# Two weight slabs side by side at the start of every dense layer

## The chip, the cores and the metric

The kernel runs on one core of a Trainium2 chip. TensorE (PE) multiplies 128x128 tiles of weights with 128x512 tiles of activations and sums in PSUM banks; VectorE (DVE), ScalarE (ACT) and GpSimd (POOL) do the elementwise work; SyncE (SP) issues most of the transfers. The metric is the device time of one execution in microseconds (us), lower is better: the median of three runs.

## The reference, cut to what matters

A token mixer, an expert layer (PEER) and two further blocks follow each other on 512 tokens of width 1024. All but the expert layer are chains of "normalise, multiply with a weight matrix, elementwise work, add to the residual". The changed code is in the multiplications with a weight matrix:

```
a = rmsnorm(h, g_mix); z = a @ w_in                                  # w_in
h = h + concat([ya, yb, yc]) @ w_out                                 # w_out
gate = sigmoid(rmsnorm(h, g) @ w_gate); h = h + gate * (p @ w_proj)  # ple_a, ple0, ple1
u = rms_norm(x) @ ssm_w_in; ...; val, gate = split(g @ w_glu)        # ssm_in, glu
up = rms_norm(x) @ w_up; c = conv(up); x = x + (gelu(g) * val) @ w_down   # up0/down0, up1/down1
k, v = split(rms_norm(x, kv_norm) @ kv_w); q = rms_norm(x) @ w_q     # w_k, w_v, attn_q
x = x + o @ w_o                                                      # attn_o
```

## The kernel before, in words

Activations lie transposed in SBUF as eight tiles (KT = 8) of 128 features by 512 tokens. A weight matrix comes in slabs: one slab holds the weights of 128 output features, eight 128x128 tiles for a depth of 1024 (ten in the three `ple` layers, where two more tiles multiply the side input `p`). `LAYERS` lists 15 layers with their numbers of slabs, 226 slabs in all.

Products are made of half-precision parts. Every operand is split into an f16 part and a bf16 remainder, and each product of two tiles is three matmuls (`PARTS`), so a slab is 24 matmuls of 512 columns, 30 in a `ple` layer. VectorE splits the activations (`split_tile`, L1171 to L1176, called by `norm_tiles`, L1204, once per tile after scaling it; each finished tile counts up `a_ready` or `x_split`). GpSimd splits the weights (`split`, L1824): L1833 writes the f16 part, L1835 the remainder, and its drain at L1836 counts up `split_done`.

A slab goes through these stations: SyncE loads it into one of four places of `wring`; GpSimd splits it into one of two places of `wsp` (NSPLIT = 2); TensorE multiplies it into bank `t % 4`; ScalarE or VectorE reads the bank and counts up `evac_done`. What holds the order of GpSimd is this wait, ahead of the split of slab `s`:

```
1832:  po.wait_ge(w_used, r * NSLOT + used(s - NSPLIT + 1))
```

`w_used` counts slabs that TensorE has begun: its first matmul adds one (L453). When slab `s - 1` has begun, slab `s - 2` is finished, and its place in `wsp` is free for slab `s`. So the second slab of a layer is split only after the first one has begun, and the third after the second has begun. Only the first two slabs of the program (of `w_in`) have no such wait.

On TensorE `plain` (L457) runs the slabs of a layer one after the other with `product` (L444), and `paired` (L474) does it for the `ple` layers, where each slab fills two banks, one with the gate (eight tiles) and one with the product with `p` (two tiles). In the first slab `product` waits for each of the eight activation tiles by itself (L448). `halves` (L489) runs `down0` and `down1`, which the change leaves alone; so does the loop for `w_v` (L735).

The stages are parted by barriers of TensorE, ScalarE and VectorE (L330). In `w_in`, `ple_a`, `ssm_in`, `up0`, `ple0`, `w_k`, `up1` and `ple1` VectorE normalises the tiles while TensorE takes them; in `w_out` it splits them without a norm. In `glu`, `attn_q` and `attn_o` the activations are all there when the layer starts.

Of the kernel before, what the change touches and what calls it, by code (L numbers as in the profile page):

```python
# [14 lines left out]
P = 128  # L15
SEQ, D = 512, 1024
KT = D // P
# [36 lines left out]
NSLOT = NBANK = 4  # L54
NSPLIT = 2
# [16 lines left out]
def build(nc, A, first=0, last=99):  # L72
# [3 lines left out]
    s = t = FIRST  # L76
# [6 lines left out]
    def used(s):  # L83

        return s - FIRST + 1
# [9 lines left out]
    PLES = [name for name in ("ple_a", "ple0", "ple1") if name in stages]  # L95
    ctx = ExitStack()
    with ctx:
# [3 lines left out]
        def sem(name):  # L101
            return ctx.enter_context(nc.semaphore(name))
# [20 lines left out]
        banks = [ctx.enter_context(nc.psum_tensor(f"bank{i}", [P, SEQ], F32)) for i in range(8)]  # L123
# [12 lines left out]
        def parts_of(arena, at, tiles, width):  # L136

            v = arena[:, at:at + tiles * width].bitcast(F16)
            return v.rearrange("p (k h n) -> p k h n", h=2, n=width)

        def low(ap):
            return ap.bitcast(BF16)

        xs = parts_of(R, 14848, KT, SEQ)
        wsp = parts_of(R, 18944, NSPLIT, WSLOT)
# [15 lines left out]
        w_used = sem("w_used")  # L161
        mm_done = sem("mm_done")
# [37 lines left out]
        s0 = 2 * RING * D + NT * D  # L200
# [33 lines left out]
        ps = parts_of(R, 3072, 2, SEQ)  # L234
        p_loaded, sg_ready, p_split = sem("p_loaded"), sem("sg_ready"), sem("p_split")
        split_done, x_split = sem("split_done"), sem("x_split")
# [194 lines left out]
        def _(pe):  # L431
# [5 lines left out]
            def free_bank(t, r, step):  # L437

                if step or t - NBANK >= FIRST:
                    pe.wait_ge(evac_done, r * step + used(t - NBANK))  # L440

            PARTS = ((0, 0), (0, 1), (1, 0))

            def product(bank, slot, k0, n, x, ready=None, base=0, start=True, stop=True, first_of_slab=True):  # L444

                for k in range(n):
                    if ready is not None:
                        pe.wait_ge(ready, base + k + 1)  # L448
                    for p, (i, j) in enumerate(PARTS):
                        w, v = wsp[:, slot, i, (k0 + k) * P:(k0 + k + 1) * P], x[:, k, j, :]  # L450
                        mm = pe.matmul(bank[:, :], low(w) if i else w, low(v) if j else v,  # L451
                                       start=(start and k == 0 and p == 0), stop=(stop and k == n - 1 and p == 2))
                        if k == 0 and p == 0 and first_of_slab:  # L453
                            mm.then_inc(w_used, 1)
                return mm

            def plain(name, x, ready=None, base=0):  # L457

                n, s0, t0, kt = SLABS[name], SLAB0[name], TILE0[name], KTILES[name]
                if s0 % NSLOT or n % NSLOT:  # L460
                    for i in range(n):
                        s, t = s0 + i, t0 + i
                        pe.wait_ge(split_done, used(s))
                        free_bank(t, 0, 0)
                        product(banks[t % NBANK], s % NSPLIT, 0, kt, x, ready if i == 0 else None, base)\
                            .then_inc(mm_done, 1)
                    return
                with pe.Fori(0, n // NSLOT) as r:
                    for u in range(NSLOT):
                        pe.wait_ge(split_done, r * NSLOT + used(s0 + u))  # L470
                        free_bank(t0 + u, r, NSLOT)
                        product(banks[u], u % NSPLIT, 0, kt, x, ready if u == 0 else None, base).then_inc(mm_done, 1)

            def paired(name, x, ready, base):  # L474

                n, s0, t0 = SLABS[name], SLAB0[name], TILE0[name]
                with pe.Fori(0, n // NSLOT) as r:
                    for u in range(NSLOT):
                        pe.wait_ge(split_done, r * NSLOT + used(s0 + u))
                        free_bank(t0 + 2 * u, r, 2 * NSLOT)  # L480
                        product(banks[2 * u % NBANK], u % NSPLIT, 0, KT, x, ready if u == 0 else None, base)\
                            .then_inc(mm_done, 1)
                        free_bank(t0 + 2 * u + 1, r, 2 * NSLOT)
                        if u == 0:
                            pe.wait_ge(p_split, PLES.index(name) + 1)
                        product(banks[(2 * u + 1) % NBANK], u % NSPLIT, KT, 2, ps, first_of_slab=False)\
                            .then_inc(mm_done, 1)

            def halves(name, x):  # L489

# [13 lines left out]
            if stage("mixer"):  # L504
                norm_stats(NORM["mixer"])
                plain("w_in", xs, a_ready, KT * NORM["mixer"])

                pe.wait_ge(evac_done, used(TILE0["w_in"] + 17))
                for T in range(NT):
                    if T >= 2:  # L510
                        pe.wait_ge(v_ev, T - 1)
                    for k in range(TC):
                        mm = pe.transpose(banks[6 + T % 2][:, k * P:(k + 1) * P], zt[:, 15 + k, T * P:(T + 1) * P],
                                          ident)
# [12 lines left out]
                for pr in range(TC):  # L527
                    if pr == 2:
                        pe.wait_ge(mix_used, 1)
                    for T in range(NT):  # L530
                        for hh in range(2):
# [3 lines left out]
                            mm = pe.matmul(out, ones_row[0:1, 0:HD], bs_row[0:1, h * P:(h + 1) * P],  # L535
                                           start=False, stop=True, tile_position=(0, hh * HD))
                    mm.then_inc(mix_mm, 1)
                barrier(pe, "mixer")
            if stage("w_out"):
                plain("w_out", xs, x_split, KT * SPLITS.index("w_out"))  # L540
                barrier(pe, "w_out")
            if stage("w_q"):
                norm_stats(NORM["w_q"])

                for T in range(NT):
                    if T >= 1:
                        pe.wait_ge(nt_ev, 2 * T)
                    for k in range(KT):
                        if T == 0:
                            pe.wait_ge(a_ready, KT * NORM["w_q"] + k + 1)  # L550
                        mm = pe.transpose(banks[6 + k // 4][:, (k % 4) * P:(k % 4 + 1) * P],
                                          aT[:, k, T * P:(T + 1) * P], ident)
# [3 lines left out]
            if stage("peer"):  # L556
# [54 lines left out]
                for k in range(KT):  # L611
                    if k >= 2:
                        pe.wait_ge(back_used, k - 1)
                    for T in range(NT):
                        mm = pe.transpose(banks[6 + k % 2][:, T * P:(T + 1) * P], acc[:, T, k * P:(k + 1) * P], ident)
                    mm.then_inc(back_mm, 1)
                barrier(pe, "peer")
            def ple(name):
                norm_stats(NORM[name])
                paired(name, xs, a_ready, KT * NORM[name])  # L620
                barrier(pe, name)

            def feed_forward(i):
                if stage(f"up{i}"):
                    norm_stats(NORM[f"up{i}"])
                    plain(f"up{i}", xs, a_ready, KT * NORM[f"up{i}"])
                    barrier(pe, f"up{i}")
                if stage(f"down{i}"):
                    halves(f"down{i}", ffz)
                    barrier(pe, f"down{i}")  # L630
# [100 lines left out]
            if stage("kv"):  # L731
# [11 lines left out]
                for T in range(NT):  # L743
                    for c in range(2):
# [3 lines left out]
                        for k in range(4):  # L748
                            mm = pe.transpose(banks[6 + c][:, k * P:(k + 1) * P], vf[:, 4 * c + k, T * P:(T + 1) * P],
                                              ident)  # L750
# [5 lines left out]
                for h in range(HEADS):  # L756
                    if h >= 2:
                        pe.wait_ge(b_ev, h - 1)
                    pe.matmul(banks[h % 2][:, 0:SKEW], relb[:, h * P:(h + 1) * P], onehot,
                              start=True, stop=True).then_inc(b_mm, 1)  # L760
# [1289 lines left out]
```

## Time and profile before

| | |
|---|---|
| median of three runs | 3698.16 us (3685.31 to 3701.19) |
| profiled execution | 3692.53 us, span in the trace 3690.8 us |
| TensorE matmul busy | 2856.3 us (77%), 9692 matmuls |
| VectorE busy | 2455.7 us (67%) |
| GpSimd busy | 1724.7 us (47%) |
| ScalarE busy | 701.4 us (19%) |
| mean granted TensorE clock | 0.867 of full speed |

A busy share is an average over stages: between the barriers another engine bounds each. In the middle of the program (about 320 to 1780 us) the expert layer runs, which the change does not touch. A row of the timeline merges instructions of one kind that follow each other; what stands in square brackets is how long the engine had been idle and who released it.

### The profile page before, as it was taken

Reading aid. Unit: us, or ns where it says so; the run is one execution under the profiler, and the core shown is the slowest. Engines: PE = TensorE matmul, PEld = TensorE weight load, DVE = VectorE, ACT = ScalarE, POOL = GpSimd, SP = SyncE. Lnnn points to the kernel's source line nnn. Section 1 sums busy time; section 2 is a strip of 40 time slices with the busy share of each in tenths; the row PEclk is TensorE's granted clock in tenths of the full one; section 3 lists DMA queues with packets and bytes.
Section 4 is the critical chain, followed back from the end, with each engine's and each line's share of the span. In section 5 each row is a group of like instructions: output and inputs, shape, how many; then the busy total and the mean of one; then the engine's idle time right before and its main releaser. Section 6 shows DMA issues by size and latency. Waiting matters only on the chain. (4 is left out here: it accounts for less than half of the span.)

```text
span 3690.8 us, 34648 instructions
## 1 busy us (share of the span) xinstructions
PE 2856.3 (77%) x9692; PEld 1295.9 (35%) x9692; DVE 2455.7 (67%) x4157; ACT 701.4 (19%) x1560; POOL 1724.7 (47%) x1030
## 2 busy tenths in 40 slices
PE   5557788787878787877556768899969855689997
PEld 2223333333333333333224653344424333234442
DVE  5966766767676766776897454775487466877645
ACT  0001222222222222222012220121011333112100
POOL 4403434434443443443336437677746300358774
PEclk9858999999999999999777659999979855789998
DMA  2201999999998999999121012233312110123331
GB/s 98 71 6 48 401 399 384 399 379 399 379 413 361 410 384 401 365 420 398 63 80 42 18 52 91 80 102 103 104 50 84 39 41 6 40 74 102 101 104 57
DMA packets 131212, 696.22 MB, mean 189 GB/s; under 512 B 29660, under 2 KB 30973, under 8 KB 64926
## 3 DMA queue, kind: packets, MB, share of 16 engines
q0 software_dynamic: 73728, 536.90, 35.6%
q1 hardware_dynamic: 57374, 158.12, 12.5%
q8 instruction: 35, 0.57, 0.1%
q14 instruction: 75, 0.61, 0.0%
HBM read 687.11 MB, written 7.86 MB: 188 GB/s over the span
## 5 line engine op out<-in xcount | busy, mean ns | idle before, releaser
L451 PE MATMUL bank<-R 128*128 128x512 f16 (+1 forms) x4800 | 1101.3, 391 | 184.3 <-DVE R L1176 101.2
L576 PE MATMUL bank<-R,Z 128*128 128x512 f32 x2048 | 997.8, 637 | 267.1 <-ACT Z L899 257.7
L1863 POOL DMA_INDIRECT R<-expert_uv_dram,idx x512 | 589.7, 1152 | 842.2 <-PE bank L576 751.8
L1833 POOL TENSOR_TENSOR R<-wring,beat 128x1024 f16<-128x1024 f32 (+2 forms) x226 | 472.6, 2091 | 973.3 <-PE bank L451 615.8
L451 PEld LDWEIGHTS bank<-R 128*128 128x128 f16 (+1 forms) x4800 | 468.4, 100 | 826.4 <-issue 198.6
L1409 DVE SCALAR_TENSOR_TENSOR R<-R 128x1024 f32<-128x1024 f32 x512 | 618.7, 1222 | 189.7 <-DMA R<-expert_uv_dram,idx 158.9
L576 PEld LDWEIGHTS bank<-R,Z 128*128 128x128 f32 x2048 | 394.6, 201 | 850.6 <-issue 552.5
L1835 POOL TENSOR_TENSOR R<-wring,R 128x1024 bf16<-128x1024 f32 (+2 forms) x226 | 550.2, 2435 | 40.0 <-issue 7.5
L899 ACT ACTIVATE Z<-consts,R 128x128 f32<-128x128 f32 x512 | 177.6, 394 | 442.2 <-DVE R L1421 436.1
L451 PE MATMUL bank<-Z,R 128*128 128x512 f16 (+1 forms) x1056 | 232.8, 384 | 11.1 <-ACTq L332 11.1
L892 ACT ACTIVATE R<-R 128x2 f32<-128x2 f32 x256 | 52.1, 204 | 540.5 <-DVEq L1411 540.2
L451 PEld LDWEIGHTS bank<-Z,R 128*128 128x128 f16 (+1 forms) x1056 | 104.3, 99 | 139.6 <-issue 18.1
L963 ACT ACTIVATE R<-bank,cols 128x512 f32<-128x512 f32 x88 | 68.4, 778 | 403.7 <-PE bank L451 403.7
L1180 DVE TENSOR_TENSOR sq<-hT 128x512 f32<-128x512 f32 (+1 forms) x72 | 128.3, 1782 | 6.1
L1538 DVE SCALAR_TENSOR_TENSOR R<-bank,cols,R 128x511 f32<-128x511 f32 x88 | 65.4, 743 | 97.4 <-ACT R L963 97.4
L1558 DVE RECIPROCAL xt<-rstd 128x512 f32<-128x512 f32 x24 | 80.4, 3351 | 67.5 <-ACT rstd L986 66.9
L1182 DVE TENSOR_TENSOR sq<-sq 128x512 f32<-128x512 f32 x72 | 121.4, 1686 | 5.4
L1225 DVE TENSOR_TENSOR hT<-hT,bank 128x512 f32 x32 | 22.0, 688 | 154.1 <-PE bank L451 153.2
L1335 DVE MEMSET R<- 128x32 f32 x32 | 2.7, 85 | 176.5 <-PE bank L563 175.4
L587 PE MATMUL bank<-aT,Z 128*128 128x512 f32 x256 | 114.4, 601 | 0.7 <-ACTq L332 0.7
L1254 DVE SCALAR_TENSOR_TENSOR R<-R,cols 128x512 f32<-128x512 f32 x90 | 93.4, 1091 | 9.6 <-issue 9.6
L1176 DVE TENSOR_TENSOR Z<-xt,Z 128x512 f32 x44 | 92.2, 2096 | 7.3 <-issue 7.3
(254 smaller groups left out, 2679.8 us busy)
## 6 DMA issues: line engine op xcount, KB each, us to landing
wring<-up_dram SPq DMA_DIRECT2D x88, 512.0 KB, 3.2
wring<-down_dram SPq DMA_DIRECT2D x32, 704.0 KB, 4.0
wring<-ple_dram SPq DMA_DIRECT2D x16, 640.0 KB, 3.9
wring<-w_in_dram SPq DMA_DIRECT2D x18, 512.0 KB, 3.4
Z<-w_q_dram SPq DMA_DIRECT2D x16, 512.0 KB, 6.5
R<-expert_uv_dram,idx POOLq DMA_INDIRECT x512, 11.4
wring<-glu_dram SPq DMA_DIRECT2D x16, 512.0 KB, 3.3
wring<-ple_a_dram SPq DMA_DIRECT2D x8, 640.0 KB, 4.9
```

What stands on the lines that cost most here:

```text
L451: mm = pe.matmul(bank[:, :], low(w) if i else w, low(v) if j else v, start=(start and k == 0 and p == 0), stop=(stop and k == n - 1 and p ...
L576: mm = pe.matmul(banks[2 * par + c][:, :], diag[:, k % 4, :], pairs[:, slot, 1, c * SEQ:(c + 1) * SEQ], start=(k == 0), stop=(k == TOPK - 1))
L587: mm = pe.matmul(banks[6 + half][:, :], wq[:, half, k * P:(k + 1) * P], aT[:, k, :], start=(k == 0), stop=(k == KT - 1))
L899: ac.activation(diag[:, k % 4, :], ident, ACT.Copy, scale=actg[:, par, k:k + 1])\
L1176: return ve.tensor_tensor(low(dst[:, 1, :]), src, dst[:, 0, :], ALU.subtract)
L1180: ve.tensor_tensor(sq[:, 1, :], x, x, ALU.mult)
L1182: ve.tensor_tensor(sumsq, sumsq, sq[:, 1, :], ALU.add)
L1254: ve.scalar_tensor_tensor(ca[:, i, :], ypad[:, i, bass.ds(j, SEQ)], cols[:, bass.ds(j * TA + (COLS["conv_a_w"] + i), 1)], ca[:, i, :], ALU ...
L1409: dot = ve.scalar_tensor_tensor(pairs[:, slot, 0, :], pairs[:, slot, 0, :], 1.0, ntok[:, T, :], ALU.mult, ALU.mult, accum_out=act[:, par, ...
L1833: po.tensor_tensor(wsp[:, slot, 0, 0:w], src, one.broadcast_to([P, w]), ALU.mult)
L1835: po.tensor_tensor(low(wsp[:, slot, 1, 0:w]), src, wsp[:, slot, 0, 0:w], ALU.subtract)
L1863: po.indirect_dma_start(pairs[:, slot, :, :].rearrange("p a b -> p (a b)"), None, A["expert_uv"], bass.IndirectOffsetOnAxis(idx[:, n % 2, ...
```

## The change

`side_by_side` takes the first two slabs of a layer together: for each activation tile it runs the three matmuls of the first slab into one bank and then the three of the second into another. In the first round it waits for the split of each slab. The first matmul of all counts up `w_used` once, and the last matmul of the first slab once more (in a `ple` layer that second count comes with the second slab's first matmul on `p`). `plain` uses it for its first two slabs and runs the others as before; `paired` too, and its loop is turned over in steps of two slabs. Both banks are reported finished together in `plain`. No engine but TensorE has other instructions, and the sum of matmuls is the same.

```
+            def side_by_side(s, outs, x, ready, base, whole=True):
+                for k in range(KT):
+                    pe.wait_ge(ready, base + k + 1)
+                    for half in range(2):
+                        if k == 0:
+                            pe.wait_ge(split_done, used(s + half))
+                        for p, (i, j) in enumerate(PARTS):
+                            w, v = wsp[:, (s + half) % NSPLIT, i, k * P:(k + 1) * P], x[:, k, j, :]
+                            mm = pe.matmul(outs[half][:, :], low(w) if i else w, low(v) if j else v,
+                                           start=(k == 0 and p == 0), stop=(k == KT - 1 and p == 2))
+                            if half == 0 and (k, p) in ((0, 0), (KT - 1, 2) if whole else (0, 0)):
+                                mm.then_inc(w_used, 1)
+                return mm
...
             def plain(name, x, ready=None, base=0):
...
+                free_bank(t0, 0, 0)
+                free_bank(t0 + 1, 0, 0)
+                side_by_side(s0, [banks[(t0 + i) % NBANK] for i in range(2)], x, ready, base)\
+                    .then_inc(mm_done, 2)
+                straight = n if s0 % NSLOT or n % NSLOT else NSLOT
+                for i in range(2, straight):
+                    s, t = s0 + i, t0 + i
+                    pe.wait_ge(split_done, used(s))
+                    free_bank(t, 0, 0)
+                    product(banks[t % NBANK], s % NSPLIT, 0, kt, x).then_inc(mm_done, 1)
...
             def paired(name, x, ready, base):
...
+                free_bank(t0 + 3, 0, 0)
+                side_by_side(s0, [banks[0], banks[2]], x, ready, base, whole=False).then_inc(mm_done, 1)
+                pe.wait_ge(p_split, PLES.index(name) + 1)
+                for half in range(2):
+                    product(banks[2 * half + 1], half, KT, 2, ps, first_of_slab=(half == 1)).then_inc(mm_done, 1 + half)
```

TensorE's instructions at the start of `glu`, before (L451 is `product`; slab 0 goes to bank0, slab 1 to bank1):

```order
L440 REGISTER_ALU [waits split_done]
L451 MATMUL bank0<-R 128x512 [waits x_split,evac_done]
L451 MATMUL bank0<-R 128x512 x2
L451 MATMUL bank0<-R 128x512 [waits x_split]
L451 MATMUL bank0<-R 128x512 x2
...
L440 REGISTER_ALU [waits split_done]
L451 MATMUL bank1<-R 128x512 [waits evac_done]
L451 MATMUL bank1<-R 128x512 x23
L470 REGISTER_ALU
L440 REGISTER_ALU [waits split_done]
L451 MATMUL bank2<-R 128x512 [waits evac_done]
```

The same place in the changed kernel (L466 is `side_by_side`):

```order
L466 MATMUL bank0<-R 128x512 [waits x_split,evac_done,split_done,stage_done]
L466 MATMUL bank0<-R 128x512 x2
L466 MATMUL bank1<-R 128x512 [waits split_done]
L466 MATMUL bank1<-R 128x512 x2
L466 MATMUL bank0<-R 128x512 [waits x_split]
L466 MATMUL bank0<-R 128x512 x2
L466 MATMUL bank1<-R 128x512 x3
...
L451 MATMUL bank2<-R 128x512 [waits evac_done,split_done]
L451 MATMUL bank2<-R 128x512 x23
```

The wait for slab 1's split has moved from behind the 24 matmuls of slab 0 to behind its first three, and the next wait for a split, that of slab 2, stands behind 48 matmuls of which the forty-third to forty-fifth are the last that read slab 0.

## Rows read from the trace of the kernel before

**Rows 1.** TensorE's waits: who it waited for, us in total, times, longest.
```profile
PE bank L576 <- ACT Z L899: 257.7, 183, 6.1
PE bank L451 <- DVE R L1176: 101.2, 61, 7.8
```

**Rows 2.** Timeline of TensorE, start of `up1`: start, us, instruction [idle before <-releaser].
```profile
3242.01 1.44 PE L451 MATMUL bank<-R 128*128 128x512 f16 x3 [6.49 <-DVE R L1176]
...
3256.89 1.46 PE L451 MATMUL bank<-R 128*128 128x512 f16 x3 [0.47 <-DVE R L1176]
3258.81 13.54 PE L451 MATMUL bank<-R 128*128 128x512 f16 x58 [0.46 <-DVE R L1176]
```

**Rows 3.** Timeline of GpSimd, start of `up1`.
```profile
3242.68 2.10 POOL L1833 TENSOR_TENSOR R<-wring,beat 128x1024 f16<-128x1024 f32 x1 [12.26 <-PE bank L451]
...
3260.78 1.89 POOL L1833 TENSOR_TENSOR R<-wring,beat 128x1024 f16<-128x1024 f32 x1 [13.48 <-PE bank L451]
3262.83 2.13 POOL L1835 TENSOR_TENSOR R<-wring,R 128x1024 bf16<-128x1024 f32 x1
3265.96 1.89 POOL L1833 TENSOR_TENSOR R<-wring,beat 128x1024 f16<-128x1024 f32 x1 [1.01 <-PE bank L451]
```

**Rows 4.** Stretches of the span: us, busy us (instructions) per engine, granted clock, DMA.
```profile
3186.00:3192.00 6.00, 5.65 (x14) 2.11 (x15) 0.48 (x1) 0.00 (x0) 4.02 (x2) 0.50 0.00 0
3261.00:3400.00 139.00, 139.00 (x645) 62.50 (x644) 98.78 (x93) 28.44 (x41) 112.03 (x54) 1.00 0.29 98
```

**Rows 5.** Timeline of TensorE, start of `glu`.
```profile
2208.31 24.04 PE L451 MATMUL bank<-R 128*128 128x512 f16 x100 [19.08 <-DVEq L332]
```

**Rows 6.** Timeline of GpSimd, start of `glu`.
```profile
2208.97 1.89 POOL L1833 TENSOR_TENSOR R<-wring,beat 128x1024 f16<-128x1024 f32 x1 [7.83 <-PE bank L451]
2211.01 2.12 POOL L1835 TENSOR_TENSOR R<-wring,R 128x1024 bf16<-128x1024 f32 x1
2216.09 1.90 POOL L1833 TENSOR_TENSOR R<-wring,beat 128x1024 f16<-128x1024 f32 x1 [2.96 <-PE bank L451]
...
2221.27 1.90 POOL L1833 TENSOR_TENSOR R<-wring,beat 128x1024 f16<-128x1024 f32 x1 [1.02 <-PE bank L451]
```

**Rows 7.** Timeline of GpSimd, start of `attn_q`: splits of slabs 1 and 3.
```profile
2866.96 1.90 POOL L1833 TENSOR_TENSOR R<-wring,beat 128x1024 f16<-128x1024 f32 x1 [1.87 <-PE bank L451]
...
2877.32 1.90 POOL L1833 TENSOR_TENSOR R<-wring,beat 128x1024 f16<-128x1024 f32 x1 [1.01 <-PE bank L451]
```

**Rows 8.** Timeline of GpSimd, start of `attn_o`: splits of slabs 1 and 3.
```profile
3187.02 1.89 POOL L1833 TENSOR_TENSOR R<-wring,beat 128x1024 f16<-128x1024 f32 x1 [56.31 <-PE bank L451]
...
3200.09 1.90 POOL L1833 TENSOR_TENSOR R<-wring,beat 128x1024 f16<-128x1024 f32 x1 [0.75 <-PE bank L451]
```

**Rows 9.** Timeline of GpSimd, start of `w_out`: splits of slabs 1 and 3.
```profile
265.61 2.22 POOL L1833 TENSOR_TENSOR R<-wring,beat 128x1024 f16<-128x1024 f32 x1 [119.98 <-PE bank L451]
...
283.43 1.90 POOL L1833 TENSOR_TENSOR R<-wring,beat 128x1024 f16<-128x1024 f32 x1 [0.76 <-PE bank L451]
```

**Rows 10.** Timeline of TensorE, last tile of `ple1`.
```profile
3633.97 16.29 PE L451 MATMUL bank<-R 128*128 128x512 f16 x70 [0.47 <-DVE R L1176]
```

**Rows 11.** Timeline of GpSimd, `ple1`: splits of slabs 2 and 3.
```profile
3637.39 2.32 POOL L1833 TENSOR_TENSOR R<-wring,beat 128x1280 f16<-128x1280 f32 x1 [14.94 <-PE bank L451]
3639.86 2.87 POOL L1835 TENSOR_TENSOR R<-wring,R 128x1280 bf16<-128x1280 f32 x1
3643.86 2.32 POOL L1833 TENSOR_TENSOR R<-wring,beat 128x1280 f16<-128x1280 f32 x1 [1.14 <-PE bank L451]
```

**Rows 12.** Timeline of TensorE in `ple_a`.
```profile
1796.38 4.36 PE L451 MATMUL bank<-R 128*128 128x512 f16 x12 [16.83 <-POOLq L1836]
...
1827.23 6.65 PE L451 MATMUL bank<-R 128*128 128x512 f16 x30 [0.91 <-DVE R L1502]
1836.28 8.34 PE L451 MATMUL bank<-R 128*128 128x512 f16 x30 [2.40 <-DVE R L1502]
```

**Rows 13.** Timeline of VectorE, first product with the gate in `ple_a`.
```profile
1813.39 0.69 DVE L1502 TENSOR_TENSOR R<-R,bank 128x512 f32<-128x512 f32 x1 [3.09 <-PE bank L451]
```

**Rows 14.** Timeline of TensorE, the instruction behind `ssm_in`.
```profile
1971.84 1.94 PE L659 MATMUL bank<-consts,R 128*128 128x128 f32 x8 [13.49 <-POOLq L1886]
```

More of the change, by code:

```diff
@@ L457, in plain @@
             def plain(name, x, ready=None, base=0):
                 n, s0, t0, kt = SLABS[name], SLAB0[name], TILE0[name], KTILES[name]
[L460 to L466, printed above, removed]
+                free_bank(t0, 0, 0)
@@ L467, in plain @@
+                if straight == n:
                     return
-                with pe.Fori(0, n // NSLOT) as r:
+                with pe.Fori(0, (n - NSLOT) // NSLOT) as r:
                     for u in range(NSLOT):
-                        pe.wait_ge(split_done, r * NSLOT + used(s0 + u))
-                        free_bank(t0 + u, r, NSLOT)
-                        product(banks[u], u % NSPLIT, 0, kt, x, ready if u == 0 else None, base).then_inc(mm_done, 1)
+                        pe.wait_ge(split_done, r * NSLOT + used(s0 + NSLOT + u))
+                        free_bank(t0 + NSLOT + u, r, NSLOT)
+                        product(banks[u], u % NSPLIT, 0, kt, x).then_inc(mm_done, 1)
@@ L474, in paired @@
             def paired(name, x, ready, base):
                 n, s0, t0 = SLABS[name], SLAB0[name], TILE0[name]
[L477 to L487, printed above, removed]
+                free_bank(t0 + 3, 0, 0)
@@ new lines, in paired @@
+                side_by_side(s0, [banks[0], banks[2]], x, ready, base, whole=False).then_inc(mm_done, 1)
+                pe.wait_ge(p_split, PLES.index(name) + 1)
+                for half in range(2):
+                    product(banks[2 * half + 1], half, KT, 2, ps, first_of_slab=(half == 1)).then_inc(mm_done, 1 + half)
+                with pe.Fori(0, (n - 2) // 2) as r:
+                    for u in range(2):
+                        pe.wait_ge(split_done, r * 2 + used(s0 + 2 + u))
+                        free_bank(t0 + 4 + 2 * u, r, 4)
+                        product(banks[2 * u], u, 0, KT, x).then_inc(mm_done, 1)
+                        free_bank(t0 + 5 + 2 * u, r, 4)
+                        product(banks[2 * u + 1], u, KT, 2, ps, first_of_slab=False).then_inc(mm_done, 1)
```

## The prediction

> **What bounds the kernel now.** I read the waits of TensorE first. The longest, on ScalarE's diagonals (257.7 us, L576), lies in the expert layer, which the change leaves alone; the second is the change's target: 101.2 us in 61 waits for the remainder part of an activation tile (L1176) [rows 1]. Next, the timeline of TensorE at the start of a layer. In `up1` it starts at 3242.01 and then does three matmuls per tile, idle 0.47 us before each group late in the ramp; after the last tile (3258.81) it runs without a gap [rows 2], and later for 139 us with 645 matmuls, 0.2155 us each at a granted clock of 1.00 (2.4 GHz); at 0.50 (1.2 GHz) 14 matmuls filled 6 us, 0.43 us each [rows 4]. So the dense layers are bound by TensorE, and a slab of 24 is worth 5.2 us. `ple_a` is the exception: there TensorE waits for VectorE's product L1502 before each slab [rows 12].
>
> Then GpSimd's timeline, which decides this case. Its split of slab 1 begins 0.66 us after the first matmul of a layer: 2208.31 to 2208.97 in `glu` [rows 5, 6]. As that matmul takes 0.43, GpSimd starts 0.23 after its end. The split lasts 4.2 us (2208.97 to 2211.01 + 2.12), in a `ple` layer 5.3 (3637.39 to 3639.86 + 2.87) [rows 6, 11]. Before the change it hides behind the 5.2 us of the slab that runs: GpSimd idles 1.01 or 1.02 us between splits [rows 3, 6, 7].
>
> **What the change does to that chain.** The count that releases slab 1's split comes with the first matmul, as before. But TensorE now wants slab 1 after three matmuls, not after 24: first hold-up. The count that releases slab 2's split comes with the last matmul on slab 0, three matmuls before both slabs are done: second hold-up, 0.23 + 4.2 + 0.15 (from GpSimd's end to TensorE, an estimate, a little under the 0.23 just read for the way back) less 3 x 0.22 = 3.9 us without a matmul. Before, that split ran beside slab 1. Saving slab 1's time and then waiting for slab 2's split is 5.2 against 3.9 at best; where no tile was waited for there is nothing to save and both hold-ups are paid.
>
> **Layers whose tiles are there at once.** I count 12 low matmuls (5.1 us, the middle of the 4 to 6 us that such starts stay at 0.50 [rows 4]) and then the high rate; after restarting there are 42 matmuls up to the release.
> - `glu`: slab 1 is split at 2213.13, restart 2213.3, then 5.1 + 30 x 0.2155 = 11.6 gives 2224.9; + 0.2 + 4.2 + 0.15 = 2229.4 for slab 2. Before: GpSimd took slab 3 at 2221.27, 0.45 after slab 2's first matmul, so 2220.8 [rows 6]. +8.6 us.
> - `attn_o`: 3187.02 + 4.35 = 3191.4, + 11.6 + 4.5 = 3207.5, against 3200.09 - 0.45 = 3199.6 [rows 8]. +7.9 us.
> - `attn_q` comes straight out of other matmuls at the high clock, but the first hold-up stops them for 4.1 us; I charge eight low ones: 2866.96 + 4.35 = 2871.3, + 8 x 0.43 + 34 x 0.2155 = 10.8, + 4.5 gives 2886.6, against 2877.32 - 0.45 = 2876.9 [rows 7]. +9.7 us.
> - `w_out`, tiles split but not normalised, all early enough: 265.61 + 4.65 (the first half of the split took 2.22 here) = 270.3, + 11.6 + 4.6 = 286.5, against 283.43 - 0.45 = 283.0 [rows 9]. +3.5 us.
>
> **Layers with a ramp.** In `up1` the first hold-up lasts from 3242.68 to about 3247.3. From then TensorE works without a pause, 12 low and 27 high matmuls, 10.9 us, and has caught up at 3258.3, before the last tile at 3258.81. Three more matmuls release GpSimd: 3258.81 + 0.65 + 0.2 + 4.2 + 0.15 = 3264.0 for slab 2, against 3265.96 - 0.45 = 3265.5 [rows 2, 3]. -1.5 us, and the same taken for `w_in`, `up0` and `w_k`, whose ramps have the same 24-matmul slabs: -6.0 us. (`w_in` has slab 1 split beforehand, so only the second hold-up.)
> In `ple1`: 3633.97 + 13 x 0.2155 (six for the tile, six on `p`, one that releases) = 3636.8, + 0.2 + 5.3 + 0.15 = 3642.5, against 3643.86 - 0.45 = 3643.4 [rows 10, 11]. -0.9, and the same for `ple0`: -1.8 us.
> `ple_a` is VectorE's: its first product waited until 1813.39 for slab 0 [rows 13]. Now 1796.38 + 0.66 + 5.3 + 0.15 = 1802.5 is the restart [rows 12]; 5.1 + 33 x 0.2155 = 12.2 gives 1814.7, six matmuls on `p` 1816.0. +2.7 us, all on the path. The late slab 2 is hidden behind VectorE's two tiles.
> `ssm_in` loses about as much as `w_out`, but the stage behind it waits 13.49 us for GpSimd, itself behind VectorE's preparation [rows 14]: 0 us. Without that cover it would be up to the 9.7 of `attn_q`.
>
> The other edits: the loops run one round less, and the waits for tiles in their later rounds, all long met, are gone. In `paired` both banks' waits come at the start, when VectorE has emptied everything. A running loop keeps its matmuls 0.2155 us apart with those waits in it [rows 4], so I take 0, with 1 us either way.
>
> Sum without the clock: 8.6 + 7.9 + 9.7 + 3.5 + 2.7 - 6.0 - 1.8 = +24.6 us.
>
> **The clock after the second hold-up.** In `ple_a` a slab of 30 took 6.65 us after 0.91 us of idleness, and 8.34 us after 2.40 us [rows 12]: an idle stretch of that size costs 1.7 us, eight matmuls at 0.50. The new pause of 3.9 us stands in ten layers (all but `ple_a` and `ssm_in`, where it is hidden): 10 x 1.7 = +17 us. The bounds are 0, if after two denser slabs the clock stays, and 2.8 us each, if it stays low as long as after a stage's start (13 matmuls by the 6 us of [rows 4]).
>
> The Trainium skill bears on this, "TensorE: Matmul & The Clock Gate", section "Loop structure matters more than you think": it wants a loop whose matmuls stay back to back while something else overlaps, and says that a long wait between groups of matmuls makes the next ones run cold. The rows agree, 8.34 against 6.65. By that rule the sum is +41.6, without it +24.6.
>
> Total: +41.6. Against the profiled execution, 3692.5 us, that is 3734 us. That execution was 5.7 us under the median of the runs, so on the median's footing it is 3698.2 + 41.6, rounded to 3739 us, 1.1% more.
>
> **Rivals.**
> 1. The clock stays up across the pauses: +24.6, 3722.5 us. For it, before the pause TensorE is busier than in the old ramps; against it, the 2.40 us in `ple_a`. Chance 0.20.
> 2. The clock does worse. Either each pause costs 2.8 us (+28 in place of +17: 3750), or it doesn't rise during the ramps, as it didn't in `up1` until the last tile. Then 42 x 0.43 = 18.1 from 3247.4 gives 3265.5 and slab 2 at 3270.0, +4.5 in place of -1.5, six ramps: +36, 3775. Against the latter, TensorE was idle for part of each tile before, and will not be now. Chances 0.10 and 0.05.
> 3. The change keeps its promise: slab 1 vanishes in the ramps, and GpSimd is not in the way because the next splits run during the ramp. Six ramps that TensorE bounds give 4 x 5.2 + 2 x 6.5 = -33.8, the layers without a ramp 0: 3664 us. That hangs on one point, whether slab 2 can be split while slab 0 is read. There are two places for split slabs, and in `up1` GpSimd stood idle 13.48 us with slab 2 loaded until TensorE released it [rows 3], which speaks against it. Chance 0.04.
> 4. What is lost at the start of `glu`, `attn_q`, `attn_o` and `w_out` is hidden by the engine that takes up the results, and only the ramps count: -7.8, 3690 us. Against it, TensorE runs from 2208.31 on without a gap [rows 5], so nothing downstream holds it. Chance 0.05.
>
> My forecast has 0.56. A measurement of this kernel tells about 0.5% (18.5 us) from no change. Slower by more: the forecast, rival 2 and 0.16 of rival 1, 0.87; within: rival 4 and the low side of rival 1, 0.04, together 0.09; faster by more: rival 3, 0.04. The range is 3714 to 3758: down to rival 1 with 8 us for the runs' own scatter, up to the 2.8 us per pause with as much.
>
> **What the profile after must show.** In `glu` three matmuls, a pause of 4 us until GpSimd's drain L1836, 45 matmuls, and a second pause of 4 us with the same releaser; waits for L1836 up by some 80 us in total, those for L1176 down by half or more; eight or so matmuls at 0.50 behind each pause; slab 2 in `up1` 1 to 2 us sooner after the last tile. The forecast is wrong if GpSimd splits slab 2 before TensorE is through with slab 0, if the pauses lie on no path that sets the end, or if the ramps save over 3 us each.

## The result and the profile after

The changed kernel takes 3736.1 us (median of five runs, 3730.38 to 3741.37) against 3699.42 us before in the same set: a ratio of 1.0101, 95% interval 1.0079 to 1.0123. It is slower by 1.0%, 37 us; 1.1% and 3739 us had been forecast. The profiled execution took 3732.55 us with a span of 3730.8, 40.0 us more than the 3690.8 before.

First TensorE's waits, who it waited for, us in total, times and longest. This is the profile after (L1856 is what L1836 was, L1196 what L1176 was, L466 is `side_by_side`):

```profile
PE bank L466 <- POOLq L1856: 87.3, 13, 26.0
...
PE bank L451 <- POOLq L1856: 49.7, 13, 5.5
...
PE bank L466 <- DVE R L1196: 38.8, 19, 7.9
...
PE bank L466 <- issue: 15.3, 2, 7.7
```

The wait for tiles that the change is about fell from 101.2 to 38.8 us [rows 1]. Part of that fall is a change of name: the last row is the wait for the first tile of `ple0` and of `ple1`, 7.65 us each, which the trace before puts down to L1176 (7.70 us each) and this one to no engine. Like for like the fall is from 101.2 to 54.1 us. The waits for GpSimd's split are now 137.0 us together, against 44.8 before (L451 waiting for L1836). The timeline of TensorE at the start of `glu` after shows both pauses:

```profile
2216.05 1.46 PE L466 MATMUL bank<-R 128*128 128x512 f16 x3 [18.51 <-DVEq L332]
2221.00 11.59 PE L466 MATMUL bank<-R 128*128 128x512 f16 x45 [3.49 <-POOLq L1856]
2236.28 5.99 PE L451 MATMUL bank<-R 128*128 128x512 f16 x15 [3.70 <-POOLq L1856]
```

and the timeline of GpSimd beside it shows why:

```profile
2216.74 1.89 POOL L1853 TENSOR_TENSOR R<-wring,beat 128x1024 f16<-128x1024 f32 x1 [6.96 <-PE bank L466]
2218.78 2.12 POOL L1855 TENSOR_TENSOR R<-wring,R 128x1024 bf16<-128x1024 f32 x1
2232.02 1.89 POOL L1853 TENSOR_TENSOR R<-wring,beat 128x1024 f16<-128x1024 f32 x1 [11.13 <-PE bank L466]
2234.05 2.12 POOL L1855 TENSOR_TENSOR R<-wring,R 128x1024 bf16<-128x1024 f32 x1
```

Where TensorE ran from 2208.31 on without a gap [rows 5], it now does three matmuls, stands until GpSimd has split slab 1, does 45, and stands again for slab 2. GpSimd, free for 11.13 us, could not begin slab 2 before the last matmul on slab 0.

A layer with a ramp, `up1`, TensorE after:

```profile
3281.27 1.44 PE L466 MATMUL bank<-R 128*128 128x512 f16 x3 [6.60 <-DVE R L1196]
3286.56 9.02 PE L466 MATMUL bank<-R 128*128 128x512 f16 x33 [3.85 <-POOLq L1856]
3296.04 1.47 PE L466 MATMUL bank<-R 128*128 128x512 f16 x6 [0.46 <-DVE R L1196]
3297.97 1.47 PE L466 MATMUL bank<-R 128*128 128x512 f16 x6 [0.46 <-DVE R L1196]
3303.14 3.17 PE L451 MATMUL bank<-R 128*128 128x512 f16 x7 [3.71 <-POOLq L1856]
```

It catches up (33 matmuls without a gap, then groups of six at the tiles' pace). Slab 2 starts 21.9 us after the first matmul, 23.5 before [rows 2, 3]: the ramp pays, 1.6 us. Then the price of the pause. Stretches after, in the columns of [rows 4]:

```profile
2236.00:2242.00 6.00, 5.72 (x15) 2.15 (x16) 3.64 (x3) 0.00 (x0) 4.83 (x3) 0.54 0.26 87
2244.00:2300.00 56.00, 56.00 (x261) 24.94 (x259) 25.35 (x20) 2.98 (x5) 46.51 (x22) 1.00 0.29 99
3303.00:3306.00 3.00, 2.85 (x7) 1.04 (x8) 2.64 (x3) 0.00 (x0) 2.05 (x3) 0.52 0.54 169
```

Behind the pause of 3.7 us the granted clock is 0.54 and 0.52; slab 2 of `glu` took 7.8 us in place of 5.2, that of `up1` 6.8 in place of 5.2.

The table is worked out from the timelines: us from a layer's first matmul to slab 2's first, and to its last matmul's end.

| layer | to slab 2: before, after | difference | whole layer: difference | forecast |
|---|---|---|---|---|
| w_in | 20.34, 18.74 | -1.60 | +1.23 | +0.2 |
| w_out | 18.02, 21.18 | +3.16 | +5.85 | +5.2 |
| ple_a | 23.30, 25.36 | +2.06 | +2.69 | +2.7 |
| ssm_in | 17.17, 22.76 | +5.59 | +4.67 | 0 for the end |
| glu | 12.50, 20.23 | +7.73 | +9.96 | +10.3 |
| up0 | 24.32, 21.84 | -2.48 | -0.80 | +0.2 |
| ple0 | 26.14, 26.34 | +0.20 | +1.90 | +0.8 |
| w_k | 24.33, 22.19 | -2.14 | -1.16 | +0.2 |
| attn_q | 10.36, 19.93 | +9.57 | +12.12 | +11.4 |
| attn_o | 13.28, 21.14 | +7.86 | +10.64 | +9.6 |
| up1 | 23.49, 21.88 | -1.61 | -0.03 | +0.2 |
| ple1 | 27.15, 26.34 | -0.81 | +0.88 | +0.8 |

Together the layers are 48.0 us longer. In this pair of executions the stretch from `w_out` to `ple_a`, the expert layer mainly, was 5.8 us shorter (1476.4 against 1482.2 us). Over the traces of this study it lies between 1476 and 1490 us without an order that goes with the kernels, so I take that as scatter.

### The profile page after: what moved, and what is told of

The parts are those of the page before. It is cut to its first block, busy times and chain, and to the rows that moved or that the text cites. A ratio compares the mean times of both kernels' runs of the same rounds, so it can differ in the third digit from the quotient of the medians.

```text
span 3730.8 us, 34523 instructions
## 1 busy us (share of the span) xinstructions
PE 2849.8 (76%) x9692; PEld 1298.3 (35%) x9692; DVE 2447.6 (66%) x4157; ACT 700.6 (19%) x1560; POOL 1721.1 (46%) x1030
## 3 DMA queue, kind: packets, MB, share of 16 engines
HBM read 687.11 MB, written 7.86 MB: 186 GB/s over the span
## 4 chain that ended last, share of the span: by engine, by line
POOLq 24%; issue 24%; DVE 16%; DMA 15%; PE 15%; DVEq 3%; ACT 1%; POOL 1%; ACTq 0%; SPq 0%
DMA R<-expert_uv_dram,idx 14%; POOLq L1856 13%; POOLq L1854 11%; PE bank L596 6%; DVE R L1429 5%; PE bank L451 4%; DVE sq L1200 1%; PE bank L729 1%; DVE sq L1202 1%; PE bank L730 1%; DVE R L1786 1%; PE bank L708 1%; DVE xt L1578 1%; ACT Z L919 1%; DVEq L1685 0%
## 5 line engine op out<-in xcount | busy, mean ns | idle before, releaser
L451 PE MATMUL bank<-R 128*128 128x512 f16 (+1 forms) x4224 | 946.3, 387 | 57.6 <-POOLq L1856 49.7
L451 PEld LDWEIGHTS bank<-R 128*128 128x128 f16 (+1 forms) x4224 | 417.5, 100 | 587.1 <-issue 68.3
L466 PE MATMUL bank<-R 128*128 128x512 f16 (+1 forms) x576 | 159.7, 439 | 170.4 <-POOLq L1856 87.3
L451 PE MATMUL bank<-Z,R 128*128 128x512 f16 (+1 forms) x1056 | 232.2, 384 | 11.1 <-ACTq L332 11.1
L466 PEld LDWEIGHTS bank<-R 128*128 128x128 f16 (+1 forms) x576 | 59.4, 109 | 277.3 <-issue 124.0
L451 PEld LDWEIGHTS bank<-Z,R 128*128 128x128 f16 (+1 forms) x1056 | 104.2, 99 | 139.2 <-issue 17.3
```

Source lines behind the costliest of these rows:

```text
L466: mm = pe.matmul(outs[half][:, :], low(w) if i else w, low(v) if j else v, start=(k == 0 and p == 0), stop=(k == KT - 1 and p == 2))
```

## The experiments

All are timed in five rounds beside the kernel before, which took 3700.67 us in the set of the first four and 3695.04 us in that of the other three; ratios are to it.

**Only the layers without a ramp put back.** `w_out`, `glu`, `attn_q` and `attn_o` run one slab after the other again:

```
             def plain(name, x, ready=None, base=0):
+                if name in ("w_out", "glu", "attn_q", "attn_o"):
+                    return one_by_one(name, x, ready, base)      # plain of the kernel before
```

> The changed kernel, but w_out, glu, attn_q and attn_o take their first two slabs one after the other again; the eight layers with a ramp stay side by side. Theory (the loss is two pauses per layer in which TensorE waits for GpSimd's split): from the two traces these four layers lost 5.9 + 10.0 + 12.1 + 10.6 = 38.6 us from first to last matmul, so the time falls from 3736 to about 3698, and each of the four has its old length to within 0.5 us. Rival (taking two slabs in turns costs by itself, in every layer, by the alternation of two banks and weights): only four of twelve layers are relieved, a third of the 37 us, about 3724.

Measured: 3702.73 us, ratio 1.0002 (0.9988 to 1.0016). The theory had 3698, the rival 3724. `glu` starts like this (TensorE's timeline):

```profile
2216.90 23.19 PE L451 MATMUL bank<-R 128*128 128x512 f16 x96 [19.10 <-DVEq L332]
```

`w_out`, `glu` and `attn_q` are within 0.2 us of their lengths before; `attn_o` is 1.0 us shorter, since it spent fewer matmuls at the low clock (slab 2 after 12.27 us, 13.28 before). So nearly all of the loss is in four layers, and in the other eight side by side is worth nothing that the time can tell (the interval is about 5 us either way). In this trace those eight are together 10.0 us longer than before, so they gave back nothing of what the change was made for.

**The pause filled.** Sixteen matmuls with a result that nobody reads stand behind the first two slabs (in `paired` too, which is not shown):

```
+            def fill(slot, x):
+                for _ in range(16):
+                    pe.matmul(banks[7][:, :], wsp[:, slot, 0, 0:P], x[:, 0, 0, :], start=True, stop=True)
...
+                fill((s0 + 1) % NSPLIT, x)
                 straight = n if s0 % NSLOT or n % NSLOT else NSLOT
```

> The changed kernel, and behind the first two slabs of every layer with side_by_side 16 matmuls into a bank that nobody reads (3.5 us at 2.4 GHz, inside the pause of 4.1 us), so that TensorE does not stand still while GpSimd splits slab 2. Theory (about half of the loss is TensorE's clock, which falls in that pause): the 13 or 14 matmuls at 0.50 behind the pause go, 1.0 to 2.8 us in each of ten layers by the two traces, 20 us together, about 3716; the start of slab 2 does not move. Rival (the slower slab 2 has another cause, such as GpSimd's or VectorE's traffic): no change, 3736, or slower by what the 16 matmuls stick out of the pause.

Measured: 3725.21 us, 1.0069 (1.0046 to 1.0092): 11 us less, where 20 were expected; the six executions scatter from 3717 to 3736 us, and the profiled one is 14.8 us shorter than that of the changed kernel. TensorE at `glu`, and a stretch over slab 2 and what follows:

```profile
2215.89 11.49 PE L471 MATMUL bank<-R 128*128 128x512 f16 x45 [3.49 <-POOLq L1863]
2227.22 3.62 PE L460 MATMUL bank<-R 128*128 128x512 f16 x16
2231.08 9.24 PE L451 MATMUL bank<-R 128*128 128x512 f16 x42 [0.25 <-POOLq L1863]
```

```profile
2216.00:2300.00 84.00, 83.75 (x380) 36.88 (x380) 37.25 (x28) 5.46 (x8) 61.07 (x29) 0.98 0.27 89
```

The start of slab 2 hardly moved (20.15 us after the first matmul, 20.23 without the fill), and slab 2 took 5.19 us in the eight layers with 24 matmuls where it had taken 6.8 to 8.0, and 6.5 in `ple0` and `ple1` where it had taken 8.2. Summed over the ten, from slab 2's first matmul to the end of the layer, that is 21.6 us, as expected: the clock term is shown, layer by layer. The largest part of what did not reach the end is in `w_v`, which follows `w_k` and became 6.2 us longer:

```profile
2831.12 2.08 PE L664 MATMUL bank<-sq,consts 128*128 128x512 f32 x2 [3.05 <-ACT sq L1008]
```

TensorE came earlier to the first group statistic of `w_v`. That waits for ScalarE, which waits for VectorE, still busy with the tiles for `attn_q`; behind the wait TensorE's next slab ran partly at the low clock (24 matmuls in 7.32 us). VectorE did not just give nothing, it became slower: its last tile was done 58.8 us after `w_k`'s first matmul, 55.5 in the changed kernel and 54.1 before. `w_k` and `w_v` together take 107.1 us, against 102.7 in the changed kernel and 103.9 before.

**Three places for split slabs**, in the changed kernel, and in the kernel before as control:

```
-NSPLIT = 2
+NSPLIT = 3
...
                     if not (isinstance(r, int) and s - NSPLIT < FIRST):
-                        po.wait_ge(w_used, r * NSLOT + used(s - NSPLIT + 1))
+                        po.wait_ge(w_used, r * ROUND12 + used(s - NSPLIT + 1))      # ROUND12 = 12
```

> The changed kernel with three places for split slabs in place of two (NSPLIT = 3; R is 640 words longer and sumsq2 has moved into Z for room; the loops over slabs are written out or go in steps of twelve). The split of slab s now waits for slab s - 2 to have begun, so slabs 0 and 1 can be split before a layer starts and slab 2 while slab 0 is read. Theory: both pauses vanish, the four layers without a ramp are as long as before the change, and the ramps keep the whole second slab, 4 x 5.2 + 2 x 6.5 = 34 us: about 3665. Rival (the pauses are only the first of several limits; VectorE and GpSimd get in each other's way in the ramp and eat the gain): no better than before the change, 3690 to 3700.

> The kernel before the change with the same three places for split slabs and the same written-out loops, as the control of the run with three places. Theory: with one slab after the other no layer waits for a split in steady state, so 3699 within 5 us. Rival (the third place is worth something by itself, because splits fall outside the ramp and leave VectorE alone): 8 ramps by up to 3 us, 3675 to 3690.

Measured: 3684.96 us, 0.9961 (0.9947 to 0.9975) with `side_by_side`; 3700.82 us, 1.0003 (0.9990 to 1.0015) without. So the third place by itself gives nothing in sum, the change by itself costs 37 us, and both together are 15 us faster than before. TensorE in `up1` with both:

```profile
3238.58 2.72 PE L467 MATMUL bank<-R 128*128 128x512 f16 x6 [6.60 <-DVE R L1199]
3241.84 1.47 PE L467 MATMUL bank<-R 128*128 128x512 f16 x6 [0.55 <-DVE R L1199]
3245.64 1.47 PE L467 MATMUL bank<-R 128*128 128x512 f16 x6 [2.33 <-DVE R L1199]
...
3255.29 1.47 PE L467 MATMUL bank<-R 128*128 128x512 f16 x6 [0.46 <-DVE R L1199]
3256.59 5.78 PE L452 MATMUL bank<-R 128*128 128x512 f16 x26
```

No pause is left here (the first one is still there in `ple_a`, 4.04 us, and `ssm_in`, 3.29): six matmuls per tile, and slab 2 follows at once, 18.0 us after the first matmul, 23.5 before. `up1` is 5.5 us shorter than before, `ple1` 5.5, `up0` 6.3, `w_in` 7.9, `w_k` 7.1, `w_out` 4.6; `glu` and `attn_q` have their old lengths to 0.1 us. All twelve layers together are 36.7 us shorter, more than the 34 of the theory, though not quite where it had them: its six ramps give 30.7 us, and `w_out` 4.6 that it had at nothing. Yet only 15 arrive. The traces show where the other 22 go, and most of it is VectorE's. `w_v` is 10.3 us longer:

```profile
2813.07 2.08 PE L661 MATMUL bank<-sq,consts 128*128 128x512 f32 x2 [7.66 <-ACT sq L1004]
```

This is VectorE between 2770 and 2800, making the tiles for `attn_q` while GpSimd splits, row by row 2.0 to 2.6 us where [rows 2]'s ramp had such tiles ready every 1.93 us; the last row is the start of the next tile, and GpSimd's row stands below:

```profile
2785.08 2.61 DVE L1230 SCALAR_TENSOR_TENSOR xt<-hT,cols,rstd 128x512 f32<-128x512 f32 x1
2787.77 1.96 DVE L1197 CAST R<-xt 128x512 f16<-128x512 f32 x1
2789.80 2.46 DVE L1199 TENSOR_TENSOR R<-xt,R 128x512 bf16<-128x512 f32 x1
2792.18 2.38 DVE L1230 SCALAR_TENSOR_TENSOR xt<-hT,cols,rstd 128x512 f32<-128x512 f32 x1
```

```profile
2787.38 2.06 POOL L1856 TENSOR_TENSOR R<-wring,beat 128x1024 f16<-128x1024 f32 x1 [0.24 <-issue]
```

The kernel before at the same work, VectorE and then GpSimd:

```profile
2789.29 2.61 DVE L1207 SCALAR_TENSOR_TENSOR xt<-hT,cols,rstd 128x512 f32<-128x512 f32 x1
...
2794.61 2.61 DVE L1207 SCALAR_TENSOR_TENSOR xt<-hT,cols,rstd 128x512 f32<-128x512 f32 x1
```

```profile
2802.66 2.15 POOL L1833 TENSOR_TENSOR R<-wring,beat 128x1024 f16<-128x1024 f32 x1 [0.65 <-PE bank L451]
```

A tile takes VectorE 7.1 us in place of 5.3: GpSimd, no longer held up by TensorE, idles 0.24 us between splits in place of 0.65 and is beside it nearly all the time. And `ple_a` and `ple0` are 2.3 and 1.6 us longer than before (counted in the 36.7), for TensorE waits there for VectorE to free banks.

Part of the leak comes with the third place, whatever the order of slabs, for the control has it too. Both kernels begin `w_in` 3.5 to 3.6 us later (43.4 and 43.3 against 39.8 us): GpSimd now splits a third slab there, while VectorE sums the squares of the input, and the 24 instructions of VectorE ahead of `w_in` are busy 27.7 us in both, 24.4 before (with `side_by_side` the third split runs from 21.4 to 26.0; a square of a tile beside it, at 24.11, takes 2.45 us, and one behind it, at 27.41, 0.69).

From the end of `w_in` to `w_out` both need 123.0 to 123.1 us where every trace with two places has 119.4 to 119.5; VectorE's convolution lies there, and the last three of its products ahead of the end of `w_in` take 7.1 us beside the denser splits in place of 5.2; that this is the reason is read from the rows and not tested. And from `attn_q` to `attn_o` both need 281.4 to 281.7 us, where traces with two places have 277.9 to 280.2 (278.3 before), again with a third slab split in between. `ssm_in`, 3.3 us shorter, brings the stage behind it on by 0.2 us only. With `w_v` that is 10.3 + 3.6 + 3.8 + 3.1 + 3.1 = 23.9 us, all that is missing and 2 more, which other stretches gave. Half of the rival's thought was right: VectorE does eat most of the gain. But not all, so its 3690 to 3700 was not reached either.

**ScalarE's tables earlier.** The one layer that I had at 0 and that cost something was `ssm_in`; the section below tells what the traces show of it. The edit, in the changed kernel and, as control, in the kernel before:

```
                 for n in range(KT):
-                    if n == NBANK:
+                    if n == 2:
                         ac.wait_ge(prep, 2)
                         ac.activation(bigM, bigM, ACT.Exp)
```

> The changed kernel, with one move on ScalarE in ssm_in: its tables of powers (exponential and sines, which VectorE waits for) stand behind the copies of two tiles of u, not of four. Theory (the slip of ssm_in reaches the end because these tables are queued behind the copy of TensorE's tile 3): VectorE had its input ready at 1934.6 and the tables began at 1947.2, so they begin at about 1935 to 1937, the first matmul behind ssm_in comes 4 to 8 us sooner counted from the start of ssm_in, limited next by TensorE's own last slab; 3736 becomes about 3730. Rival (the slip comes through TensorE's barrier at the end of ssm_in, at 1967, or through the way of u through memory): nothing moves.

> The kernel before the change with the same earlier tables, as the control of that run. Theory: there VectorE's input came last (ScalarE waited 5.0 us for it at 1941.1), so the move gives nothing, 3700 within 3 us. Rival (tables behind two copies are better in any case): the same 4 to 8 us as in the changed kernel.

Measured: 3735.97 us, 1.0114 (1.0095 to 1.0133) in the changed kernel, 3699.33 us, 0.9999 (0.9985 to 1.0013) in the one before. In time neither moves, so the 6 us expected of the first did not come. ScalarE in the changed kernel with the edit:

```profile
1940.04 1.06 ACT L1025 ACTIVATE R<-R 128x1024 f32<-128x1024 f32 x1 [7.95 <-DVEq L1636]
```

The tables begin 27.4 us after the layer's first matmul in place of 36.1, and the next stage's first matmul comes after 66.4 in place of 69.2 us (65.1 before the change). That is 2.8 of the 4.1 us of slip, so in the traces the queue behind ScalarE's copies is a part of it; the barrier alone, the rival, would have let nothing move. In the control the next stage comes after 65.0 us, as before. 2.8 us is below what the times can tell, and it rests on one trace. Other traces say the same of the queue: in the changed kernel, in the run with four layers put back and in that with the pause filled the tables begin after 36.1, 36.4 and 33.8 us, and the next stage comes 33.1 us behind them in all three. Before the change it came 30.7 us behind them. So 1.7 of the 4.1 us are tables that begin later, and 2.4 are VectorE's work behind the tables, which became slower: `ssm_in` ends 4.7 us later, and GpSimd's last split for it, over at 1952.8 before, lasts until 1961.9 now. The same instruction of VectorE before, then after:

```profile
1953.24 0.75 DVE L1624 TENSOR_SCALAR R<-R,consts 128x1024 f32<-128x1024 f32 x1
```

```profile
1959.98 2.46 DVE L1644 TENSOR_SCALAR R<-R,consts 128x1024 f32<-128x1024 f32 x1
```

Also, VectorE's input came 3.9 us later after the first matmul than without the edit (27.4 against 23.5 us), so that the tables gained 8.7 us of a possible 12.6.

**The choice of layers.** Three places, side by side in seven layers, and the earlier tables:

```
+                if name in ("glu", "attn_q", "attn_o"):
+                    return one_by_one(name, x, ready, base)
...
+                if name in ("ple_a", "ple0"):
+                    return paired_one_by_one(name, x, ready, base)
...
+                    if n == 2:                                   # ScalarE's tables, ssm_in
```

> Three places for split slabs, side by side only where it paid in that run (w_in, w_out, ssm_in, up0, w_k, up1, ple1), one after the other in glu, attn_q, attn_o, ple_a and ple0, and the earlier tables in ssm_in. Theory: ple0 loses 1.6 us less than with side_by_side and ple_a up to 2, the tables give 3 to 6, so from 3685 to about 3677. Rival (VectorE bounds these stretches whatever the order of slabs): as with three places in all layers, 3685.

Measured: 3684.35 us, 0.9964 (0.9948 to 0.9981), the same as with `side_by_side` everywhere; the 8 us expected did not come. `ple0` came out 0.8 us shorter than with `side_by_side` in all layers. `ple_a` came out 3.7 us longer, at 79.8 us; one slab after the other had taken it 73.8 to 77.0 us in the three other traces of that order, so this stays open. And the earlier tables did not help. TensorE in `ssm_in`, and ScalarE:

```profile
1959.94 12.10 PE L452 MATMUL bank<-R 128*128 128x512 f16 x48 [9.17 <-ACT Z L1072]
```

```profile
1953.04 1.06 ACT L1064 ACTIVATE R<-R 128x1024 f32<-128x1024 f32 x1 [21.00 <-DVEq L1675]
```

Now TensorE is so early that ScalarE stands 21.00 us in its wait for VectorE with tiles to copy behind it, all four banks fill, and TensorE stands 9.17 us. Most of that is hidden: the next stage comes 66.6 us after the layer's first matmul, 64.9 with three places and the tables in their old place. The times do not tell the two versions apart, so the simpler one, three places and `side_by_side` in all layers, is the one to keep, 0.4% faster than before.

## Why the prediction was right, point by point

1. **Two pauses per layer, both for GpSimd's split.** Right, in place and size. TensorE's waits for the split rose by 92 us where some 80 were forecast; those for tiles fell by 47% like for like, where half or more was. In `glu` the second lasts 3.70 us by the profile against 3.9 forecast; the first 3.49 us. Put back in four layers, the loss went with them; with a third place for split slabs it turned into a gain.
2. **Slab 2's start.** Forecast and measured: `glu` +8.6 and +7.73, `attn_o` +7.9 and +7.86, `attn_q` +9.7 and +9.57, `w_out` +3.5 and +3.16, `up1` -1.5 and -1.61, `ple1` -0.9 and -0.81. Taking `up1` for its three likes was a little too careful: `up0` -2.48, `w_k` -2.14, `w_in` -1.60. Taking `ple1` for `ple0` was not: `ple0` +0.20, forecast -0.9. Before the change `up0` and `w_k` had eight low matmuls behind the ramp, which the new order lacks.
3. **The clock term.** Forecast 1.7 us in each of ten layers, 17 in all; measured by filling the pause, 21.6 us in the profiled execution. The mechanism was right and the size low in this trace: in five of the ten (`w_in`, `w_out`, `glu`, `attn_q`, `attn_o`) the clock stayed at 0.50 for about 13 matmuls in place of eight, 2.5 to 2.8 us each, the upper bound I had given. The size is not fixed, though. The run with the tables earlier has the same TensorE program, and by the same measure its trace gives 16.8 us: there slab 2 of `attn_q` lost nothing behind the same pause. TensorE and the granted clock in that trace, then the clock in the changed kernel at the same place:

```profile
2900.72 11.61 PE L451 MATMUL bank<-R 128*128 128x512 f16 x53 [3.71 <-POOLq L1856]
```

```profile
2901.00:2906.00 5.00, 5.00 (x25) 2.29 (x24) 0.00 (x0) 0.00 (x0) 4.02 (x2) 1.00 0.30 105
```

```profile
2902.00:2907.00 5.00, 5.00 (x12) 1.77 (x13) 0.00 (x0) 0.00 (x0) 4.01 (x2) 0.50 0.32 105
```

The row that I took the 1.7 us from is as uneven: in `ple_a` of the kernel before with three places an idle stretch of 2.45 us cost nothing once and 1.7 us the next time.

```profile
1845.65 6.63 PE L452 MATMUL bank<-R 128*128 128x512 f16 x30 [2.45 <-DVE R L1501]
1854.74 8.32 PE L452 MATMUL bank<-R 128*128 128x512 f16 x30 [2.45 <-DVE R L1501]
```

So a price per pause holds for a sum over ten pauses, not for one. Rival 1 (no clock term) is refuted by the stretch at 0.54.
4. **The rate in the ramp.** Rival 2's second half, a clock that stays down through the ramp, did not happen: in `up1` 33 matmuls took 9.02 us, and TensorE caught up.
5. **`ple_a`.** +2.7 forecast, +2.69 measured. VectorE's first product waited 5.68 us where it had waited 3.09 [rows 13]:

```profile
1817.02 0.69 DVE L1522 TENSOR_TENSOR R<-R,bank 128x512 f32<-128x512 f32 x1 [5.68 <-PE bank L451]
```

6. **`ssm_in` was the step that failed.** I had read the 13.49 us that TensorE waits behind it [rows 14] as cover, because it ended with GpSimd and VectorE. But VectorE was itself waiting for ScalarE's tables, and those stand in ScalarE's program behind the copy of TensorE's tile 3. ScalarE before, then after:

```profile
1935.08 1.07 ACT L1013 ACTIVATE Z<-bank 128x512 f32<-128x512 f32 x1 [4.71 <-PE bank L451]
1941.14 1.06 ACT L1005 ACTIVATE R<-R 128x1024 f32<-128x1024 f32 x1 [5.00 <-DVEq L1616]
```

```profile
1946.33 1.06 ACT L1033 ACTIVATE Z<-bank 128x512 f32<-128x512 f32 x1 [4.12 <-PE bank L451]
1947.19 1.06 ACT L1025 ACTIVATE R<-R 128x1024 f32<-128x1024 f32 x1
```

and TensorE behind the layer, after:

```profile
1980.29 1.94 PE L679 MATMUL bank<-consts,R 128*128 128x128 f32 x8 [12.92 <-POOLq L1906]
```

Before, ScalarE waited 5.00 us for VectorE ahead of the tables; after, it comes late itself, straight from the copy. TensorE's wait behind the layer is 12.92 us, hardly shorter than 13.49, though the layer is 4.7 us longer: the wait moved along and covered nothing. The cost was 4.1 us to the next stage's first matmul, where I had put it at 0; 1.7 of it are the later tables, 2.4 VectorE's slower work behind them. The total hid it: the clock term (+4.6 over its forecast) and this one (+4.1) met the shorter expert layer of the profiled pair (-5.8) and starts of slab 2 that came a little sooner than forecast (-2.0 over the ten layers). That the sum of 41.6 came so close to the 40.0 of the profiled pair is in part luck; the medians differ by 36.7 us. (On the median's footing 3698.2 + 41.6 is 3739.8, not the 3739 that I wrote.)

7. **Rival 3, the kept promise.** It named the point that decides, whether slab 2 can be split while slab 0 is read. With two places it can't. With three it can, and the six ramps then save 30.7 of the 33.8 us that rival 3 said, though the whole program gets 15.
8. **Rival 4** (the loss hidden by the engine downstream) is out for these four layers, for putting them back gave the loss back, but its mechanism is real in `w_v`.

## What to carry to other kernels

Before two blocks of work are interleaved to fill an engine's waits, ask when the buffer of the first is given back: here interleaving made TensorE want the second slab 21 matmuls sooner and give the first one back 20 later, and with two buffers the supplier, 80% busy in steady state, lost its overlap at both ends. The same edit turned from 1.0% slower to 0.4% faster with a third buffer, which alone gave nothing. And a wait in the trace is cover only if the chain that ends it does not start at the engine one delays: follow it back through each engine's program order, not just to the last releaser.

## What the runs showed of the hardware

In the profiled execution of the changed kernel a pause of 3.7 to 4.5 us between dense matmuls put the granted clock to 0.50 in every one of the ten layers, for 8 to 13 matmuls; in another trace with the same pauses it stayed at 1.00 in one of the ten (`attn_q`, 3.71 us). 16 matmuls put into the pause, with work of no use, kept it at 1.00 and made each next slab 1.6 to 2.8 us shorter. And the ramp of `up1` with three places, six matmuls per 1.93 us and 0.46 us idle each time, held the high level from its second tile to the end (1.00 from 3241.5 to 3257), where the ramp before, three per tile, ran at 0.50; in `up0` and `w_k` the ramp before did rise, at its fifth tile.

VectorE's time for one and the same instruction depended on whether GpSimd was splitting: the square of a tile took 2.45 us beside a split and 0.69 without, and a tile (three instructions) 1.93 us in a ramp without splits, 5.3 beside splits 0.65 us apart, and 7.1 beside splits 0.24 us apart. So in `w_k` and `w_v` VectorE became slower with whatever made GpSimd's splits denser, the third place as well as the filled pause.
